# Two feed-forward blocks: up-projections as seven half-size products in place of eight, activations stored, down-projections behind them in two passes

## The reference, cut to what matters

```
D_MODEL = 1024; SEQ = 1024; D_FF = 2816; FFN_CONV = 3
h = rms_norm(x, ffn_norm)
up = causal_dwconv(h @ w_up, conv_w, conv_b)      # (1024, 1024) @ (1024, 5632), then 3 taps over time
gate, value = split_cols(up, [D_FF, D_FF])
x = x + (jax.nn.silu(gate) * value) @ w_down      # (1024, 2816) @ (2816, 1024)
```

## Time and profile before

| | |
|---|---|
| median of 3 executions | 2657.23 us (2654.53 to 2663.79) |
| the profiled execution | 2656.38 us |
| its span, first to last instruction | 2654.6 us |
| TensorE busy | 2586.6 us, 97% of the span |
| VectorE busy | 1314.1 us, 50% |
| ScalarE busy | 826.1 us, 31% |
| first feed-forward phase | from 523.1 us |
| second feed-forward phase | 1941.2 us to the end |

### The profile page before, as it was taken

One profiled execution on the slowest core, in us unless ns is written; L12 is line 12 of the kernel. 1 busy time (PEld: TensorE's weight loads), 2 busy tenths in 40 slices (PEclk: granted clock), 3 DMA queues, 4 the chain that ended last, 5 costly groups with the idle time before them and its releaser, 6 DMA issues. The chain is left out here.

```text
span 2654.6 us, 32762 instructions
## 1 busy us (share of the span) xinstructions
PE 2586.6 (97%) x12444; PEld 2191.6 (83%) x12444; DVE 1314.1 (50%) x2222; ACT 826.1 (31%) x1772; POOL 196.7 (7%) x269
## 2 busy tenths in 40 slices
PE   7999889999999999999999999998999999999999
PEld 7997677888888888888899888887888888888887
DVE  4433463354444555546544552446754444444555
ACT  6434443332222222215325433324432222222221
POOL 1110220000000000001211111113000000000000
PEclk9999998999999999999999999999999999999999
DMA  4321201121111111102102101203421111111111
GB/s 141 97 72 30 103 1 56 44 85 48 48 47 47 47 47 50 52 32 103 50 16 77 33 32 56 72 1 122 134 83 54 48 48 47 47 47 47 47 40 64
DMA packets 166764, 153.90 MB, mean 58 GB/s; under 512 B 33992, under 2 KB 137400, under 8 KB 166648
## 3 DMA queue, kind: packets, MB, share of 16 engines
q1 hardware_dynamic: 162488, 152.34, 18.1%
q10 hardware_dynamic: 4160, 0.02, 0.1%
HBM read 134.71 MB, written 17.63 MB: 57 GB/s over the span
## 5 line engine op out<-in xcount | busy, mean ns | idle before, releaser
L365 PE MATMUL psum<-hT_hi,f_up_hi 128*128 128x512 f32 x1376 | 426.7, 389 | 0.6 <-PEq L585 0.6
L365 PE MATMUL psum<-hT_hi,f_up_lo 128*128 128x512 f32 x1376 | 426.3, 389 | 0.0
L365 PE MATMUL psum<-hT_lo,f_up_hi 128*128 128x512 f32 x1376 | 426.2, 389 | 0.0
L245 DVE TENSOR_TENSOR f_up_lo<-raw,f_up_hi 128x1024 fp32r<-128x1024 f32 x84 | 103.0, 1226 | 489.6 <-ACT f_up_hi L187 489.6
L365 PEld LDWEIGHTS psum<-hT_hi,f_up_hi 128*128 128x128 f32 x1376 | 258.1, 188 | 55.2 <-issue 1.7
L365 PEld LDWEIGHTS psum<-hT_hi,f_up_lo 128*128 128x128 f32 x1376 | 258.3, 188 | 53.8
L365 PEld LDWEIGHTS psum<-hT_lo,f_up_hi 128*128 128x128 f32 x1376 | 258.3, 188 | 53.6
L263 DVE TENSOR_TENSOR XY<-XY,psum 128x512 f32<-128x512 f32 x352 | 234.6, 685 | 112.4 <-PE psum L54 112.2
L187 ACT ACTIVATE f_up_hi<-raw 128x1024 fp32r<-128x1024 f32 x84 | 89.2, 1062 | 610.2 <-PE psum L365 588.9
L52 PE MATMUL psum<-f_down_hi,f_act_hi 128*128 128x512 f32 x640 | 249.0, 389 | 0.0
L53 PE MATMUL psum<-f_down_lo,f_act_hi 128*128 128x512 f32 x640 | 249.0, 389 | 0.0
(11 more groups left out here) (325 smaller groups left out, 4079.0 us busy)
## 6 DMA issues: line engine op xcount, KB each, us to landing
raw<-in_ffn_w_up_dram SPq DMA_DIRECT2D x88, 512.0 KB, 3.7
f_down_raw<-in_ffn_w_down_dram SPq DMA_DIRECT2D x22, 1024.0 KB, 4.9
w_raw<-in_b_w_in_dram SPq DMA_DIRECT2D x18, 1024.0 KB, 6.0
w_raw<-in_a_w_in_dram SPq DMA_DIRECT2D x8, 768.0 KB, 5.8
group_out<-stage SPq DMA_DIRECT2D x24, 256.0 KB, 2.3
XY<-in_x_dram SPq DMA_DIRECT2D x8, 512.0 KB, 10.3
w_raw<-in_xa_w_kv_dram SPq DMA_DIRECT2D x8, 512.0 KB, 3.5
o_w_stage<-in_a_w_out_dram SPq DMA_DIRECT2D x4, 1024.0 KB, 8.8
```

The costliest lines, as they stand in the source:

```text
L245: nc.vector.tensor_tensor(up_lo[n_slot][:, :, :], up_raw[n_slot], up_hi[n_slot][:, :, :].bitcast(F32), ALU.subtract).then_inc(up_split, 1)
L365: mm = nc.tensor.matmul(psum[:, 2 * j + half, :], w[j][:, d, :], h[:, d, half * HALF:(half + 1) * HALF], start=first, stop=final)
```

## The change

Chunks 0 and 1 (`PLAIN = 2`) stay as they were. In each of the other 20 chunks the 2 x 2 block product is done by Strassen's scheme in Winograd's form: the weight of gate and value is cut into four 512 x 128 blocks (L11, L12 for gate, L21, L22 for value), the tokens into four blocks of 512 x 512 (by half of the model width and half of the tokens). Seven products of 4 x 3 = 12 matmuls take the place of eight: P1 and P2 on L11 and L12, P6, P7, P5, P3 on sums of weight blocks (S2, S3, S1, S4), P4 on L22. P6, P7, P5, P4 use sums of token blocks (T2, T3, T1, T4), which are made once for a phase from the columns of the norm, kept in `G` (eight tiles that lie in the residual's place). The residual goes to DRAM (`x_mid`) in `out_phase` and comes back before the adds.

VectorE makes the four weight sums of a chunk (`make`), six low parts (`low`), and puts the results together from the products (`mix_step`, seven additions, each reading one PSUM bank); ScalarE makes six high parts and copies P1 out. The products rotate through all eight banks. The convolution now reads the result from SBUF (`up.room`). The activation goes to DRAM in float32 (`act_d`). The down-projections stand behind all of the up-projections, in two passes of 11 steps (`n` = 0 to 10 for tokens 0 to 511, 11 to 21 for the rest), each accumulating in the eight banks; a step is 4 x 2 x 2 x 3 = 48 matmuls, and for it 1 MB of weights and 0.5 MB of activations are loaded and split again. VectorE adds 16 blocks of 512 columns for a phase, 8 behind each pass. The norm of tokens 0 to 511 stands at the border of the passes of `f0`. The loops are written out.

The diff, cut to its core (the removed lines are those of the kernel before; the last piece is in `out_phase`):

```diff
+P1, P6, P2, P7, P5, P4, P3 = range(7)
+S2, L1, S3, S1, L22, S4 = range(6)
+M1, M2, M3, M4 = range(4)
+U2, C11, U3, U4, C22, C21, C12 = range(7)
+T2, T3, T1, T4 = range(4)
...
+        places = {S2: (s_hi[:, 0, :, :], s_lo[:, 0, :, :], sums_b), L1: (up.hi[0][:, :, :], up.lo[0][:, :, :], up_raw[0]),
+                  S3: (s_hi[:, 1, :, :], s_lo[:, 1, :, :], L21), S1: (up.hi[1][:, 0:DH, :], up.lo[1][:, 0:DH, :], sums_a),
+                  L22: (up.hi[1][:, DH:DC, :], up.lo[1][:, DH:DC, :], L22_raw), S4: (s_hi[:, 2, :, :], s_lo[:, 2, :, :], L12)}
+        read_last = {S2: P6, L1: P2, S3: P7, S1: P5, L22: P4, S4: P3}
...
+            def load_up(c):
+                for j in range(2):
+                    if c == 2:
+                        sp.wait_ge(up_split, j + 1)
+                    if c > 2:
+                        sp.wait_ge(op_split, operand(c - 1, S4))
+                    raws.load(sp, j, up_unit(w_up, j, c))
...
+            load_up(2)
+            store_act(0)
+            for c in range(PLAIN, FC):
+                if c + 1 < FC:
+                    load_up(c + 1)
+                else:
+                    load_down(0)
+                store_act(c - 1)
+            load_down(1)
+            store_act(FC - 1)
             if begin:
...
+                sp.wait_ge(op_split, operand(FC - 1, S4))
                 begin.load(sp)
+            for n in range(2, LAST + 1):
+                load_down(n)
+                if n in (4, 7):
+                    load_rows(n // 7)
...
         @block.scalar
...
+            for c in range(PLAIN, FC):
+                more = c + 1 < FC
+                high(c, S4)
+                conv(c - 1, 0)
+                act.wait_ge(p_done, product(c, P1))
+                if c > PLAIN:
+                    act.wait_ge(mixed, mix(c - 1, C11))
+                nc.scalar.activation(p1, bank(c, P1), ACT.Copy).then_inc(copied, 1)
+                silu(c - 1)
+                if more:
+                    high(c + 1, S2)
+                    high(c + 1, L1)
+                if more:
+                    high(c + 1, S3)
+                    high(c + 1, S1)
+                    high(c + 1, L22)
+                else:
+                    both(0)
+                conv(c, 1)
+            conv(FC - 1, 0)
+            both(1)
+            silu(FC - 1)
...
+                act.wait_ge(prod_done, FC)
+                for t in range(2):
+                    square(t)
+                    norm.act_scale(act, t, X[:, t, :])
+                norm.act_high(act, 0)
+                square(2)
+                norm.act_scale(act, 2, X[:, 2, :])
+            high_down(PASS + 1)
+            if norm:
+                norm.act_high(act, 1)
+                square(3)
+                norm.act_scale(act, 3, X[:, 3, :])
+            high_act(PASS + 1)
+            if norm:
+                norm.act_high(act, 2)
+                norm.act_high(act, 3)
...
         @block.vector
...
+            for c in range(PLAIN, FC):
+                more = c + 1 < FC
+                if c > PLAIN:
+                    mix_step(c - 1, C12)
+                low(c, S4)
+                taps_of(c - 1, 1)
+                taps_of(c - 1, 0)
+                mix_step(c, U2)
+                if more:
+                    make(c + 1, M1)
+                    make(c + 1, M2)
+                multiply(c - 1)
+                mix_step(c, C11)
+                if more:
+                    low(c + 1, S2)
+                    low(c + 1, L1)
+                mix_step(c, U3)
+                if more:
+                    make(c + 1, M3)
+                    make(c + 1, M4)
+                    low(c + 1, S3)
+                mix_step(c, U4)
+                mix_step(c, C22)
+                if more:
+                    low(c + 1, S1)
+                mix_step(c, C21)
+                if more:
+                    low(c + 1, L22)
+                else:
+                    low_down(0)
+                    low_act(0)
+            mix_step(FC - 1, C12)
+            taps_of(FC - 1, 1)
+            taps_of(FC - 1, 0)
+            low_down(1)
+            low_act(1)
+            multiply(FC - 1)
...
+            for c in range(PLAIN, FC):
+                for i, (left, op, right) in enumerate(products):
+                    pe.wait_ge(op_split, operand(c, op))
+                    if c == PLAIN and i in (P6, P7, P5, P4):
+                        pe.wait_ge(t_split, {P6: T2, P7: T3, P5: T1, P4: T4}[i] + 1)
+                    m = number(c, i)
+                    if m < BANKS:
+                        pe.wait_ge(conv_done, 2 * (m // 4) + 2)
+                    else:
+                        wait_read(pe, m - BANKS)
+                    for d in range(DH):
+                        last = split_matmul(nc, bank(c, i), left[0][:, d, :], left[1][:, d, :], right[0][:, d, :], right[1][:, d, :],
+                                            d == 0, d == DH - 1)
+                    last.then_inc(p_done, 1)
...
+            for n in range(PASS):
+                wait_split(n)
+                for t in range(4):
+                    for half in range(2):
+                        if n == 0:
+                            wait_read(pe, (ALL - 1 - (2 * t + half)) // BANKS * BANKS + 2 * t + half)
+                        last = down(n, t, half, n == 0, n == PASS - 1)
+                        if n == PASS - 1:
+                            last.then_inc(out_done, 1)
+                    if norm and n == PASS - 1 and t >= 2:
+                        norm.pe(pe, t - 2)
+                if n < PASS - 1:
+                    last.then_inc(b_done, 1)
+            wait_split(PASS)
+            for t in (6, 7, 4, 5):
+                if norm and t < 6:
+                    pe.wait_ge(norm.gained, t - 1)
+                for half in range(2):
+                    i = 2 * (t - 4) + half
+                    pe.wait_ge(x_added, i + 1)
+                    last = down(PASS, t, half, True, False)
+                if norm and t >= 6:
+                    norm.pe(pe, t - 4)
...
+            for t in range(4, TT):
+                for half in range(2):
+                    down(LAST - 1, t, half, False, False)
+                    down(LAST, t, half, False, True).then_inc(out_done, 1)
+                if norm and t > 4:
+                    norm.pe(pe, t - 1)
...
+            def gained(t):
+
+                if t:
+                    dve.wait_ge(x_stored, 16 * t)
+                norm.dve_gain(dve, t)
+                norm.dve_low(dve, t)
```

More of the change, by code:

```diff
@@ new lines, in ffn_phase @@
+        if begin:
+            with ExitStack() as same_place:
+                begin.open(nc, same_place, ctx, ph)
+        ups = [up.room[:, j, :] for j in range(2)]
+        conv_out = [sb(f"conv_{n}", [P, SEQ]) for n in ("gate", "value")]
+        act_out = [sb(f"act{i}", [P, SEQ]) for i in range(2)]
+        with ExitStack() as same_place:
+            T_raw = sb("T_raw", [P, 4, DH, HALF], F32, same_place)
+        T_lo = sb("T_lo", [P, 4, DH, HALF], F32R)
+        p1, u2, u3, u4 = (sb(n, [P, HALF])[:, :] for n in ("p1", "u2", "u3", "u4"))
@@ L151, in ffn_phase @@
+        a_hi, a_lo = ([x[s][:, :, :].rearrange("p d n -> p (d n)").rearrange("p (k n) -> p k n", k=2) for s in range(2)] for x in (up.hi, up.lo))
+        ALL = product(FC - 1, P3)
         block = ctx.enter_context(nc.Block())
@@ new lines, in mix_step @@
+            def mix_step(c, i):
+                out, x, prod, made_by = steps[i]
+                dve.wait_ge(p_done, product(c, prod))
+                if i == C11:
+                    dve.wait_ge(conv_done, 2 * c)
+                if made_by is None:
+                    dve.wait_ge(copied, copy(c))
+                else:
+                    dve.wait_ge(mixed, mix(c, made_by))
+                nc.vector.tensor_tensor(out, x, bank(c, prod), ALU.subtract if i == C21 else ALU.add).then_inc(mixed, 1)
@@ new lines, in _ @@
+            mix_step(FC - 1, C12)
[4 more added lines that the diff above has]
+            multiply(FC - 1)
+            for n in range(2, PASS):
+                low_down(n)
+                low_act(n)
+                if begin and n == 4:
+                    begin.low_parts(dve)
+            add(0)
+            add(1)
+            low_down(PASS)
+            add(2)
+            add(3)
+            low_act(PASS)
+            add(4)
@@ L318, in ffn_phase @@
+            add(6)
+            add(7)
+            norm_step(1)
+            low_down(PASS + 1)
+            norm_step(2)
+            low_act(PASS + 1)
+            norm_step(3)
+            for n in range(PASS + 2, LAST + 1):
+                low_down(n)
+                low_act(n)
+            for t in range(TT // 2, TT):
+                add(2 * t)
+                add(2 * t + 1)
+                if t > TT // 2:
+                    norm_step(t - 1)
+            norm_step(TT - 1)
         if norm:
@@ new lines, in down, with wait_split @@
+            def down(n, t, half, start, stop):
+                s = n % 2
```

(17 more changed lines are left out.)

603 lines of the change are left out of this document (350 added, 253 removed).

## The result

| | before | after |
|---|---|---|
| median of 4 executions | 2657.22 us | 2585.22 us (2580.85 to 2589.64) |
| ratio | | 0.9726, 95% interval 0.9701 to 0.975 |
| the profiled execution | 2656.38 us | 2585.62 us |
| f0, from TensorE's first matmul to that of the next phase | 523.10 to 1251.47: 728.4 us | 524.87 to 1218.37: 693.5 us |
| f1, to the end of the span | 1941.19 to 2654.6: 713.4 us | 1911.58 to 2583.8: 672.2 us |

The change saves 72.0 us by the medians and 70.8 between the two profiled executions. The forecast was 2564, 21 us too low; the time lies inside the stated range.

The account below looks back on a forecast made before the run. TensorE was taken to bound the kernel: 2656.4 - 108.8 for removed matmuls + 15.4 for edges = 2563.0, with the median 0.9 above, 2564 us. The stated range was 2549 to 2604 us.

Parts of the forecast that it names:

- What bounds the kernel: Whole kernel: TensorE, busy 2586.6 of 2654.6 us; each matmul removed is worth 0.2267 us while TensorE stays fed.
- the first step: Up chunks of both phases: 480 matmuls removed, at 0.2267 us each, 108.8 us.
- VectorE in a chunk: Changed up chunk: 22 instructions and their dependences take 17.7 us against TensorE's 19.04, so TensorE keeps the bound.
- the dependence behind P3: VectorE in a chunk: a low part waits for a copy that starts with the mixing step, 0.15 us.
- no overlap: Rival, VectorE in a chunk: instruction durations add up, 19.3 us a chunk; 2576 us, chance 0.10.
- every instruction awaited: Rival, VectorE in a chunk: each instruction pays its duration and 0.15, 21.9 us a chunk; 2678 us, slower, chance 0.03.
- ScalarE's terms: ScalarE in a chunk: copies and two convolution starts, 8.5 us of 19.04, no wait later than VectorE's use.
- Loads: Raw weight pair for the next chunk: lands in 5.3 us together, needed after 5.6; covered, narrowly.
- The edges: Phase starts, up to down, pass border and tails: stalls of 12 us in f0 and 3.4 in f1, 15 given back.
- step 2: Down-projections: loads queued behind the last activation's store, parts ready after 24 us against 23.2; stall 1, in f0 3.5.
- Tails: End of each phase: last adds and norm of tokens 512 to 1023 keep their pattern, more matmuls between tiles; costs nothing.
- the edges are worse: Rival: border in f0 and phase starts each cost a whole step, 10.9 us, 33 for 15; 2590 us, chance 0.12.

Follow-up runs that it names:

- the last step apart: Changed kernel with step 21 of the second pass no longer interleaved with step 20, so TensorE waits for step 21's parts only behind step 20: 2573.70 us.
- the three added stalls: Changed kernel with TensorE in f1 waiting at steps 13, 15 and 17 for the parts of the step after: 2614.12 us, one execution.

## Why the prediction was right, and by what it was off

**What bounds the kernel: right.** The eighth product put back costs 111.6 us for the 108.8 of the first step.

**VectorE in a chunk: right to 0.2.** 17.7 us of instructions and 1.3 of waiting while TensorE sets the pace, as worked out from start-to-start distances; at its own pace VectorE takes 17.9. The term that was too small is the dependence behind P3: booked at 0.15, it is then a wait of 0.63 for a copy that stands behind another of ScalarE's instructions. The section "The DRAIN you can't avoid" of the page "VectorE: DVE Perf Modes" of the Trainium skill does not say only that the next operation waits until the pipeline has emptied; it goes on that one that is not held starts earlier. The prediction took up the first sentence alone. The trace agrees with the second: in the chunk above two mixing steps start 0.60 us apart and last 0.68. Had the durations added up, the wait could not have been 1.3. The rival "no overlap" is out, and so is "every instruction awaited".

ScalarE's terms, as listed, add up to 9.2 us and not 8.5; the trace has one activation of 1024 columns less and 8.3 to 8.4 us. Nothing hangs on it. In the rival "every instruction awaited", 21.9 against 21.76 in 40 chunks is 5.6 us more, not 4.

**Loads: right, and as narrow as said.** Three waits in 40, 1.0 us in all.

**The edges: right in most places, wrong in one that was left out.**

| edge | predicted | measured idle |
|---|---|---|
| chunk 2, each phase | 1.0 | 0.18 |
| step 0, each phase | 1.4 | 1.40 |
| step 2, f0 and f1 | 3.5 and 1.0 | 3.80 and 1.72 |
| border in f0 | 6 | 5.2 |
| step 20, each phase | "Tails ... Nothing" | 5.52 |

Without step 20 the idle time is 25.0 - 11.0 = 14.0 us against the 15.4 of the sum. That it comes so near is in part luck: chunk 2 was booked too high, and step 2 rests on a slip. Its listed terms add up to 22.2 us and not 24, which would be before the 23.2 and no wait. In f1 the parts were ready 25.1 us after the last product, since the first copy began 7.0 us after the loads were issued and the parts took 5.4 from there, not 4.2; the wait there ran from 1.58 to 2.90 us in the executions that left this place as it was. At the border tile 3 was late (3.64) and the last blocks of step 11 held (1.59), but tile 2 was not late.

**The step that failed is "Tails: the last adds and the norm of tokens 512 to 1023 keep their pattern, with more matmuls between tiles than before. Nothing."** The diff shows the interleaving of steps 20 and 21; what was not asked is whose buffer the second of them needs. With two buffers the parts of step 21 can't be made before step 19 has ended, and TensorE asks for them at just that moment. The parts take 5.5 us by the same rows that priced step 0. The experiment with the last step apart removes both stalls.

**The second term that was missing is the clock.** The sum counted idle time at its own length. At a stall of 5.52 us TensorE's clock fell to its lower level in all seventeen such waits of the seven traces that have them, and the matmuls behind lost 1.4 to 3.1 us each time. In the two phases that is 5.7 us of the change's time; the three added stalls show the same price.

With 11.0 and 5.7 the working would have given 2581. Most of the rest of the 21 us lies outside the two phases (5.3 us): 2.6 right behind f0, at a wait that the prediction did not look at, and the rest with its cause open. The measured 2585 is nearer to the rival "the edges are worse" (2590) than to the forecast, but not for that rival's reason: neither the border nor the start of a phase cost a whole step.

## What to carry to other kernels

When an instruction stream is at over 90% of the bounding engine, price it by start-to-start distances between neighbours and count its dependences one by one; durations would have shown no room here, and the room was 1.1 us of 19. Read that room from a stretch in which the stream is not waiting for the bounding engine: its idle time there, 1.3 us, hid a wait of another kind. Where a change interleaves two steps of a double-buffered pipeline, ask when the buffer of the second is released: it is the moment at which the first should start. An idle time of TensorE of some 5 us is to be booked at 7 to 9.

## What the runs showed of the hardware

The granted clock fell to 0.5 during or right after every TensorE wait of 5.52 us, seventeen in all. The matmuls behind it, 0.43 us apart and not 0.2267 while it lasted, lost 1.4 to 3.1 us. It also fell at all six of 3.80 to 5.68 us in front of step 2. Shorter waits were mixed: of seven of 3.64 or 3.65 us at the border it fell at six; 2.87 and 2.90 fell; 2.65 did not; 2.37 fell in one execution and 2.38 did not in another; 2.19 did not, 1.94 fell in one phase and 1.93 did not in the other. A whole chunk's rhythm with a wait of 1.0 us in each of 17 chunks never lowered it. So the length of the wait alone does not decide; what does was not tried.

Loads of 512 KB landed in 3.7 us in the median where they came one by one. In pairs issued 0.4 us apart the first landed in 3.8 and the second in 4.9, with activation stores on the same queue. What the stores have to do with it was not tried.
